# The memory cross-attention stage of a hybrid decoder step: seven half-block products for the query, sample values in four column strips, key rows fetched earlier

## The chip, the cores and the metric

The kernel runs on one core of one Trainium2 chip. Its time is the device time of one execution in microseconds (us). One launch computes everything; nothing is computed on the host.

## The reference, cut to what matters

One layer of a decoder serves a prompt (512 tokens) and eight sample sequences of four tokens (32 tokens) with the same weights. The 544 tokens go through every projection together. Everything is float32. The part that the change touches is the second residual step:

```python
def memory_attention(h, mk, mv, w_mq, w_mo):
    B, T, _ = h.shape
    q = (h @ w_mq).reshape(B, T, MEM_HEADS, MEM_HEAD_DIM)
    s = jnp.einsum('bthd,bmhd->bhtm', q, mk).astype(jnp.float32) * MEM_SCALE
    p = jax.nn.softmax(s, axis=-1).astype(mv.dtype)
    return jnp.einsum('bhtm,bmhd->bthd', p, mv).reshape(B, T, MEM_W) @ w_mo

x = x + memory_attention(rmsnorm(x, norm_mem_g), mk, mv, w_mq, w_mo)
```

The model width is 2048, and there are 4 memory heads of 128 over 256 memory tokens. The prompt's keys and values are computed from `mem_prompt` by `w_mk` and `w_mv`; each of the eight sample sequences reads its own from `cache_mem_k` and `cache_mem_v` (256 rows of 512 floats, 512 KB, for each sequence and kind). After this comes the gated feed-forward part (width 5632).

## The kernel before, in words

Every engine has its own instruction list, written out by hand, and the engines meet only at counting semaphores. So each engine works strictly in its own order, and whatever stands behind a waiting instruction waits too. Activations lie transposed, features on the 128 partitions and 544 tokens along the free dimension, cut into two halves of 272 tokens (`HALF`), because one PSUM bank holds 512 floats. A float32 matmul leaves two records in the trace.

Weights stream through a ring of four slabs of 1 MB (`RING`, semaphores `s_slab` when loaded and `s_used` when free). All loads of this stage are issued by SyncE, in program order: the four slabs of `w_mk`, of `w_mv`, of `w_mq` (line 857), of `w_mo` (line 861), each behind the use of the slab that it replaces; then the key rows of the eight sample sequences in two buffers `KMR` (line 867), then their value rows in six buffers `VMR` (line 874), then the small rows of the feed-forward part.

TensorE's order in the stage:

- the products for the prompt's keys and values (line 1512), each 64 matmuls of 512 columns, and two groups of transposes of the keys (line 920 is the helper of all transposes);
- the query product: `groups(1, SGR["mq"], ...)`, which for each of four 128-column slabs of `w_mq` runs 16 x 2 matmuls of 272 columns (line 925); ScalarE copies each result to `QM` (line 2026);
- `mem_scores(0)` (line 1540), `sample_keys(0)` (the transposes of the first sequence's keys, behind their load), `mem_scores(1)`, `sample_keys(1)`, `sample_scores(0)` (line 1581), and then for each of four blocks of 128 prompt tokens `mem_values` (transposes of the softmax), more sample keys and scores, and `mem_products` (line 1563);
- the softmax of the samples' scores and two transposes of it;
- the samples' value products (line 1625): for each of eight sequences, 4 heads x 2 halves of the memory, one matmul of 128 columns whose output is 32 partitions of a bank, the 32 partitions from `32 * (b % 4)` on; each sequence's products stand one behind the other. VectorE copies the bank of four sequences (line 2844), TensorE transposes it (`rows_out`), and ScalarE or VectorE copies that to `QM`;
- the output product by `w_mo` (line 1646), and on to the feed-forward part (line 956).

VectorE and ScalarE serve both streams. For `mem_scores(u)` VectorE takes the largest (`mem_largest`, line 2801), ScalarE the exponentials (`mem_exps`, line 2032), VectorE the scaling (`mem_scaled`, line 2807). Between these stand, in fixed places, the copies of the transposed sample keys (`keys_turned`, lines 1748 on ScalarE and 2154 on VectorE).

The input projection already uses, for three of its five groups, a Strassen-Winograd form: a product of a 2x2 block matrix of weights (two halves of the model width by two column tiles) with a 2x2 block matrix of activations (two halves of the width by two halves of the tokens) in seven half-block products instead of eight. `input_product` issues one of them (8 matmuls of 272 columns). Its sums are made by VectorE: of tokens in `QTS`, of weights by `input_weight_sums` in `QWS`; `input_first`, `input_middle` and `input_last` add up the results from PSUM, with the first copied by ScalarE to `QX`. Products rotate over six banks (`q_bank`), guarded by `s_qq` and `s_qx`.

## Time and profile before

| | us |
|---|---|
| median of 3 executions | 3250.27 (3248.58 to 3251.92) |
| the profiled execution, own time | 3249.63 |
| its span in the trace | 3248.0 |
| TensorE busy | 3139.9 |
| memory stage, last product of the output projection to first product by w_mo | 1261 to 1449 |
| query product in it | 58.9 |
| samples' value products in it | 13.1 busy |

The busy time of an engine is a share of the whole span; what a stage is worth is read from the timeline of that stage. The granted clock of TensorE over the whole execution is 0.988 of its full speed. The profiled execution's time lies 1.6 us above its span and 0.6 us below the median.

### The profile page before, as it was taken

The page shows a single profiled execution, that of the slowest core. Times are in us where ns is not written, and L with a number is a line of the kernel's source. Part 1 is how long each engine was busy: PE and PEld are TensorE (multiplying, and loading weights), DVE is VectorE, ACT ScalarE, POOL GpSimd, SP SyncE. Part 2 cuts the span into 40 slices and gives each one's busy share as a digit, 9 for nine tenths or more (in the row PEclk, how much of TensorE's full clock was granted, in tenths as well). Part 3 has the DMA queues.
Part 4 walks back from the last instruction along what each step waited for, and adds up shares of the span by engine and source line. Part 5 has one row for each costly group of instructions (what it writes and reads, how often), then busy time and mean ns, then how long its engine had stood idle before and what let it go on. Part 6 is the DMA issues. An engine that isn't in the chain of part 4 may idle for free.

```text
span 3248.0 us, 41139 instructions
## 1 busy us (share of the span) xinstructions
PE 3139.9 (97%) x14592; PEld 2528.6 (78%) x14592; DVE 1657.2 (51%) x3410; ACT 368.9 (11%) x899; POOL 77.8 (2%) x128
## 2 busy tenths in 40 slices
PE   8999999899888999989999999999999999999998
PEld 7788877788545886668888888888888888888876
DVE  7799232354556433136545544544454545455556
ACT  3000021111443002021000000000000000000013
POOL 0000000100012000000000000000000000000001
PEclk9999999999999999999999999999999999999999
DMA  7122223331118422631222321232232213213212
GB/s 229 53 77 67 79 66 105 118 122 48 52 30 284 156 79 95 226 123 66 90 65 72 107 81 58 84 104 77 65 92 89 90 52 103 83 55 108 86 49 94
DMA packets 299056, 306.92 MB, mean 94 GB/s; under 512 B 12680, under 2 KB 281612, under 8 KB 297023
## 3 DMA queue, kind: packets, MB, share of 16 engines
q1 hardware_dynamic: 293562, 280.38, 27.4%
q0 software_dynamic: 5376, 24.98, 2.2%
q8 instruction: 71, 1.16, 0.1%
q14 instruction: 47, 0.39, 0.0%
HBM read 291.36 MB, written 23.14 MB: 97 GB/s over the span
## 4 chain that ended last, share of the span: by engine, by line
PE 76%; DVE 2%; ACT 1%; issue 1%; DMA 0%; POOLq 0%; POOL 0%; DVEq 0%; SPq 0%; ACTq 0%
PE ps L956 58%; PE ps L1282 5%; PE ps L920 2%; PE ps L1646 2%; PE ps L925 2%; PE ps L1512 2%; PE ps L1321 1%; PE ps L1309 0%; PE ps L1310 0%; PE ps L1625 0%; ACT xT_region_b L1930 0%; PE ps L1251 0%; ACT xT_region_b L1748 0%; PE ps L1365 0%; PE ps L1563 0%
## 5 line engine op out<-in xcount | busy, mean ns | idle before, releaser
L956 PE MATMUL ps<-xT_region_b,weight_ring 128*128 128x272 f32 x2080 | 490.9, 392 | 1.1 <-DVE weight_ring L2186 1.1
L956 PEld LDWEIGHTS ps<-xT_region_b,weight_ring 128*128 128x128 f32 x2080 | 395.1, 190 | 82.9 <-issue 1.5
L956 PE MATMUL ps<-region_c,weight_ring 128*128 128x272 f32 x1664 | 401.4, 392 | 0.0
L956 PEld LDWEIGHTS ps<-region_c,weight_ring 128*128 128x128 f32 x1664 | 315.7, 190 | 65.3 <-issue 0.6
L925 PE MATMUL ps<-xT_region_b,weight_ring 128*128 128x272 f32 x1536 | 353.6, 393 | 2.7 <-DVE region_c L2154 1.1
L925 PEld LDWEIGHTS ps<-xT_region_b,weight_ring 128*128 128x128 f32 x1536 | 291.3, 190 | 63.6 <-issue 3.9
L956 PE MATMUL ps<-region_f 128*128 128x272 f32 x1408 | 336.9, 392 | 0.0
L956 PEld LDWEIGHTS ps<-region_f 128*128 128x128 f32 x1408 | 267.5, 190 | 55.1
L956 PE MATMUL ps<-region_f,weight_ring 128*128 128x272 f32 x960 | 229.9, 392 | 0.0
L1760 ACT ACTIVATE ext<-ps 128x272 f32<-128x272 f32 x100 | 39.7, 397 | 1625.9 <-PE ps L956 1614.0
L956 PEld LDWEIGHTS ps<-region_f,weight_ring 128*128 128x128 f32 x960 | 182.3, 190 | 37.7 <-issue 0.2
L2300 DVE SCALAR_TENSOR_TENSOR rstd<-ext,tile_taps,rstd 128x512 f32<-128x512 f32 x240 | 180.5, 752 | 8.5
L956 PE MATMUL ps<-region_c,region_f 128*128 128x272 f32 x704 | 177.4, 393 | 0.3 <-DVE region_f L2190 0.3
L956 PE MATMUL ps<-xT_region_b,v_tok 128*128 128x272 f32 x704 | 168.5, 392 | 0.0
L2212 DVE TENSOR_TENSOR ext<-ps,ext 128x272 f32<-128x272 f32 x100 | 44.1, 441 | 226.7 <-PE ps L956 226.7
L2210 DVE TENSOR_TENSOR ext<-ps,ext 128x272 f32<-128x272 f32 x100 | 44.1, 441 | 222.1 <-PE ps L956 222.0
L956 PEld LDWEIGHTS ps<-region_c,region_f 128*128 128x128 f32 x704 | 133.1, 190 | 29.5 <-issue 1.7
L956 PEld LDWEIGHTS ps<-xT_region_b,v_tok 128*128 128x128 f32 x704 | 133.8, 190 | 27.6
L956 PE MATMUL ps<-region_c,v_tok 128*128 128x272 f32 x480 | 119.1, 392 | 0.0
L920 PEld LDWEIGHTS ps<-consts,xT_region_b 128*128 128x128 f32 (+3 forms) x480 | 57.0, 145 | 65.1 <-issue 31.2
L956 PEld LDWEIGHTS ps<-region_c,v_tok 128*128 128x128 f32 x480 | 91.2, 190 | 18.8
L920 PE MATMUL ps<-consts,xT_region_b 128*128 128x128 f32 (+3 forms) x480 | 72.0, 290 | 31.9 <-ACT weight_ring L1748 10.6
(393 smaller groups left out, 3609.9 us busy)
## 6 DMA issues: line engine op xcount, KB each, us to landing
weight_ring<-in_w_ffn_gate SPq DMA_DIRECT2D x44, 1024.0 KB, 5.0
weight_ring<-in_w_ffn_up SPq DMA_DIRECT2D x44, 1024.0 KB, 5.0
weight_ring<-in_w_in SPq DMA_DIRECT2D x36, 1024.0 KB, 5.2
weight_ring<-in_w_ffn_down SPq DMA_DIRECT2D x64, 512.0 KB, 4.1
weight_ring<-in_w_out SPq DMA_DIRECT2D x16, 1024.0 KB, 5.3
weight_ring<-in_w_ffn_down SPq DMA_DIRECT2D x32, 384.0 KB, 3.7
region_f<-in_cache_k_cmp SPq DMA_DIRECT2D x64, 128.0 KB, 2.0
region_f<-in_cache_v_cmp SPq DMA_DIRECT2D x64, 128.0 KB, 2.0
```

Of the source, the lines that this page charges most:

```text
L920: return pe.transpose(dst, src, IDENT[0:n, 0:n])
L925: mm = pe.matmul(PS[:, 2 * j + h, 0:HALF], lhs(kt), rhs(kt, h), start=(kt == 0), stop=(kt == n - 1))
L956: mm = pe.matmul(prod(k, r), lhs[:, t, :], rhs[:, t, :], start=(t == 0), stop=(t == m - 1))
L1282: mm = pe.matmul(PS[:, 3 * f + r, 0:rhs.shape[1]], lhs, rhs, start=first, stop=last)
L1321: return pe.matmul(PS[:, 5, :], pieces[m][2], PT_[m][0:pieces[m][1], :], start=(m == 0), stop=(m == len(pieces) - 1))
L1512: mm = pe.matmul(PS[:, 2 * kind + tt, :], MT[:, kt, tt * P:(tt + 1) * P], w[:, a, :], start=(kt == 0), stop=(kt == KT - 1))
L1646: mm = pe.matmul(PS[:, n % 6, 0:HALF], w[:, kt, j * P:(j + 1) * P], QM[:, kt, h * HALF:(h + 1) * HALF], start=(kt == 0), stop=(kt == MH - 1))
L1760: act.activation(X1, prod(k, 0), ACT.Copy).then_inc(s_part, 1)
L2210: dve.tensor_tensor(U3, prod(k, 3), U2, ALU.add).then_inc(s_quad, 1)
L2212: dve.tensor_tensor(U4, prod(k, 4), U2, ALU.add).then_inc(s_quad, 1)
L2300: loop.tick(dve.scalar_tensor_tensor(out=RS[:, 0:SEQ], in0=E[:, w:w + SEQ], scalar=taps[:, w:w + 1], in1=RS[:, 0:SEQ], op0=ALU.mult, op1=A ...
```

## The change

1. The query product by `w_mq` is made by two pairs of seven half-block products (`query_pair`), with the helpers of the input projection, as its products 6 and 7. VectorE makes the sums of tokens (`MQT`, from the normed activations, one of them in place) and of weights (`MQW`) and adds up the results straight into `QM`; ScalarE makes two copies instead of four. The clearing of `QMP` moves behind this work.
2. The key rows of the first two sample sequences go to buffers of their own (`KMR`, at other places than before), and their loads are issued ahead of the slabs of `w_mq`. Those of the other six stay behind `w_mo`.
3. The value rows have eight buffers instead of six. The first six loads are issued behind the last key load, the last two behind all sample scores (they lie where the turned keys lie). The value products run head by head and half by half over four sequences in turn, in four column strips, and both turns to rows (`rows_out`) follow at the end.

```diff
-        KMR = [flat(RF, 4864 + 1024 * s, 2, MEMW) for s in range(2)]
+        KMR = [flat(RC, 9344, 2, MEMW), flat(EXA, 0, 2, MEMW)]
+        MQT = [flat(RF, 2176 * s, 8, HALF) for s in range(3)]
+        MQW = [flat(RF, 6528, 1024), flat(RF, 7552, 1024), flat(VTF, 0, 1024)]
+        QMEM = 6
-        VMR = [flat(RB, at, 2, MEMW) for at in (4096, 5120, 6144, 7168, 0, 1024)]
+        VMR = [flat(RB, at, 2, MEMW) for at in (4096, 5120, 6144, 7168, 0, 1024, 2048, 3072)]
...
+            def key_rows_in(b):
+                sp.dma_start(KMR[b % 2], A["cache_mem_k"][0, b].rearrange("(t p) h d -> p t (h d)", p=P)).then_inc(s_kmr[b % 2], 16)
+
+            key_rows_in(0)
+            sp.wait_ge(s_nac, KT - 1)
+            key_rows_in(1)
             for j in range(4):
                 sp.wait_ge(s_used[j], SGR["mq"])
...
+            for b in range(2, NB):
+                sp.wait_ge(s_tr, ms_at(b - 2) + 2)
+                key_rows_in(b)
+            sp.wait_ge(s_qp, PRODUCTS * (QMEM + 2))
             for b in range(NB):
...
-                if b >= 6:
-                    sp.wait_ge(s_mpv, QB + b - 5)
-                sp.dma_start(VMR[b % 6], ...).then_inc(s_vmr[b % 6], 16)
-
-            sp.wait_ge(s_mpv, QB + NB)
+                if b == 6:
+                    sp.wait_ge(s_mks, NB)
+                sp.dma_start(VMR[b], ...).then_inc(s_vmr[b // 4], 16)
+
+            sp.wait_ge(s_mpv, QB + 2)
...
+            pe.wait_ge(s_mke, 2)
+
+            def query_pair(k):
+                q, top, bottom = QMEM + k, RING[:, 2 * k, :], RING[:, 2 * k + 1, :]
+                pe.wait_ge(s_slab[2 * k], 16 * (SGR["mq"] + 1))
+                input_product(q, 0, top[:, 0:1024], lo[:, :, 0:HALF])
+                input_product(q, 1, top[:, 1024:2048], hi[:, :, 0:HALF])
+                pe.wait_ge(s_qsum, 6)
+                pe.wait_ge(s_qws, 4 * q + 2)
+                input_product(q, 2, MQW[1], MQT[1])
+                pe.wait_ge(s_slab[2 * k + 1], 16 * (SGR["mq"] + 1))
+                pe.wait_ge(s_qsum, 7)
+                pe.wait_ge(s_qws, 4 * q + 3)
+                input_product(q, 3, bottom[:, 0:1024], lo[:, :, HALF:TOK])
+                input_product(q, 4, MQW[0], MQT[0])
+                pe.wait_ge(s_qsum, 8)
+                input_product(q, 5, bottom[:, 1024:2048], MQT[2])
+                pe.wait_ge(s_qws, 4 * q + 4)
+                input_product(q, 6, MQW[2], hi[:, :, HALF:TOK], slabs=(2 * k, 2 * k + 1))
+
+            query_pair(0)
+            query_pair(1)
             turned(pe, end_of("memk"))
-            pe.wait_ge(s_mke, 2)
-            groups(1, SGR["mq"], PGR["mq"], KT, P, hrhs(HTL))
-            for j in range(4):
-                pe.wait_ge(s_ps[j], PGR["mo"])
+            pe.wait_ge(s_qx, QMEM + 2)
+            pe.wait_ge(s_qq, PRODUCTS * (QMEM + 2))
...
-            for b in range(NB):
-                pe.wait_ge(s_vmr[b % 6], 16 * (b // 6 + 1))
-                place = b % 4 * SAMP
+            for quarter in range(2):
+                pe.wait_ge(s_vmr[quarter], 64)
                 for h in range(MH):
                     for st in range(2):
-                        mm = pe.matmul(PS[place:place + SAMP, 2 + b // 4, ...], ..., VMR[b % 6][...], ...)
+                        for s in range(4):
+                            mm = pe.matmul(PS[s * SAMP:(s + 1) * SAMP, 2 + quarter, ...], ..., VMR[4 * quarter + s][...], ...)
                 mm.then_inc(s_mpv, 1)
-                if b == 4:
-                    rows_out(0)
+            rows_out(0)
             rows_out(1)
...
-            for j in range(4):
-                act.wait_ge(s_used[j], SGR["mq"] + 1)
-                act.activation(halves(QM[:, j, :]), PAIR[j], ACT.Copy).then_inc(s_ps[j], 1)
+            for q in (QMEM, QMEM + 1):
+                act.wait_ge(s_qq, PRODUCTS * (q - 1) + 2)
+                act.wait_ge(s_qp, PRODUCTS * q + 1)
+                act.activation(QX, q_bank(q, 0), ACT.Copy).then_inc(s_qx, 1)
...
             normed(KT, lambda kt: HTL[:, kt, :], lambda kt: XT[:, kt, :], lambda kt: VEC[:, kt, 1:2])
+            dve.wait_ge(s_h, HBASE["ffn"])
+            b11, b12, b21, b22 = [HTL[:, 8 * j:8 * j + 8, h * HALF:(h + 1) * HALF] for j in range(2) for h in range(2)]
+            dve.tensor_tensor(MQT[0], b12, b11, ALU.subtract).then_inc(s_qsum, 1)
+            dve.wait_ge(s_qsum, 5)
+            dve.tensor_tensor(MQT[1], b22, MQT[0], ALU.subtract).then_inc(s_qsum, 1)
+            dve.tensor_tensor(b12, b22, b12, ALU.subtract).then_inc(s_qsum, 1)
+            dve.wait_ge(s_qsum, 6)
+            dve.tensor_tensor(MQT[2], b21, MQT[1], ALU.subtract).then_inc(s_qsum, 1)
+            input_weight_sums(QMEM, MQW)
             turned_tiles("memk", mem_job)
-
+            input_first(QMEM)
+            input_middle(QMEM)
+            input_last(QMEM)
+            input_weight_sums(QMEM + 1, MQW)
+            input_first(QMEM + 1)
+            input_middle(QMEM + 1)
+            input_last(QMEM + 1)
             own.step(dve.memset(QMP, 0.0))
-            for j in range(4):
-                dve.wait_ge(s_ps[j], PGR["mo"])
+            dve.wait_ge(s_qq, PRODUCTS * (QMEM + 2))
```

## Rows read from the trace of the kernel before

**Rows 1.** Page of the profile: busy time by engine, and the chain that ended last.
```profile
PE 3139.9 (97%) x14592; PEld 2528.6 (78%) x14592; DVE 1657.2 (51%) x3410; ACT 368.9 (11%) x899; POOL 77.8 (2%) x128
...
PE 76%; DVE 2%; ACT 1%; issue 1%; DMA 0%; POOLq 0%; POOL 0%; DVEq 0%; SPq 0%; ACTq 0%
```

**Rows 2.** Timeline, TensorE, memory stage: start, duration, [idle before <- releaser].
```profile
1324.77 1.04 PE L920 MATMUL ps<-consts,region_c 128*128 128x128 f32 x8
1326.91 58.91 PE L925 MATMUL ps<-xT_region_b,weight_ring 128*128 128x272 f32 x256 [1.10 <-DVE region_c L2154]
1386.62 1.97 PE L1540 MATMUL ps<-region_c 128*128 128x256 f32 x8 [0.81 <-ACT region_c L2026]
1392.86 1.97 PE L920 MATMUL ps<-consts,region_f 128*128 128x128 f32 x8 [4.28 <-DMA region_f<-in_cache_mem_k]
1394.62 3.62 PE L1540 MATMUL ps<-region_c 128*128 128x256 f32 x8
...
1401.10 1.26 PE L920 MATMUL ps<-consts,region_f 128*128 128x128 f32 x8 [1.15 <-DVE region_f L2807]
...
1430.03 0.64 PE L1581 MATMUL ps<-xT_region_b,region_f 128*32 128x256 f32 x8
...
1433.61 8.52 PE L1625 MATMUL ps<-xT_region_b,region_f 128*32 128x128 f32 x80 [0.47 <-ACT region_f L1748]
...
1442.65 4.62 PE L1625 MATMUL ps<-xT_region_b,region_f 128*32 128x128 f32 x48
```

**Rows 3.** Stretches of TensorE: length, busy (records), granted clock, DMA share, GB/s.
```profile
367.00:418.60 51.60, 51.60 (x226) 1.00 0.28 82
1392.00:1398.30 6.30, 5.44 (x18) 0.50 0.41 141
1433.50:1436.20 2.70, 2.59 (x14) 0.50 0.00 0
```

**Rows 4.** Line 1414 alone (strips of the attention stage), same columns.
```profile
1024.58:1028.20 3.62, 3.62 (x132) 1.00 1.00 338
1042.40:1047.00 4.60, 4.58 (x88) 0.50 1.06 384
```

**Rows 5.** Timeline, VectorE, seven-product stretch of the input projection.
```profile
400.07 0.44 DVE L2371 TENSOR_TENSOR region_c<-ps,v_tok 128x272 f32<-128x272 f32 x1 [3.23 <-PE ps L1176]
400.43 1.22 DVE L2335 TENSOR_TENSOR region_c<-weight_ring 128x1024 f32<-128x1024 f32 x1
```

**Rows 6.** Timeline, VectorE, memory stage.
```profile
1301.84 11.22 DVE L2172 SCALAR_TENSOR_TENSOR xT_region_b<-xT_region_b,vecs,rstd 128x544 f32<-128x544 f32 x16
...
1326.70 0.91 DVE L2792 MEMSET region_f<- 128x1024 f32 x1 [0.16 <-issue]
...
1398.28 1.23 DVE L2801 TENSOR_REDUCE stats<-ps 128x4 f32<-128x1024 f32 x1 [2.72 <-PE ps L1540]
...
1399.82 1.23 DVE L2807 TENSOR_TENSOR region_f<-region_f,stats 128x1024 f32<-128x1024 f32 x1
...
1507.15 2.42 DVE L2890 TENSOR_TENSOR xT_region_b<-xT_region_b 128x2176 f32<-128x2176 f32 x1
```

**Rows 7.** Timeline, ScalarE, memory stage.
```profile
1324.97 1.03 ACT L2018 ACTIVATE region_c<-ps 128x1024 f32<-128x1024 f32 x1 [26.75 <-PE ps L1512]
...
1394.63 1.28 ACT L2032 ACT_TABLE_LOAD   x1
1395.92 0.47 ACT L2032 ACTIVATE region_f<-ps,stats 128x256 f32<-128x256 f32 x1
```

**Rows 8.** Timeline, SyncE's DMA issues: first issue, time to the last one, count.
```profile
1304.37 20.97 SPq L857 DMA_DIRECT2D weight_ring<-in_w_mq  x4
...
1386.26 32.51 SPq L867 DMA_DIRECT2D region_f<-in_cache_mem_k  x8
```

**Rows 9.** Issue to landing of the eight loads of sample value rows.
```profile
DMA to landing us min/median/max: 3.5/7.0/9.9
```

**Rows 10.** Issue to landing of the four slabs of w_mo.
```profile
DMA to landing us min/median/max: 4.9/9.0/25.1
```

More of the change, by code:

```diff
@@ L590, in hybrid_step @@
         s_kmr = [sem(f"memory_key_rows{k}") for k in range(2)]
-        s_vmr = [sem(f"memory_value_rows{k}") for k in range(6)]
+        s_vmr = [sem(f"memory_value_rows{k}") for k in range(2)]
         AT = flat(RC, 0, 8, TOK)
@@ L862, in _ @@
                              w_tiles(A["w_mo"][0])[:, :, j * 512:(j + 1) * 512]).then_inc(s_slab[j], 16)
+            for b in range(2, NB):
+                sp.wait_ge(s_tr, ms_at(b - 2) + 2)
+                key_rows_in(b)
+            sp.wait_ge(s_qp, PRODUCTS * (QMEM + 2))
             for b in range(NB):
[L865 to L876 removed]
+                if b == 6:
+                    sp.wait_ge(s_mks, NB)
+                sp.dma_start(VMR[b], A["cache_mem_v"][0, b].rearrange("(t p) h d -> p t (h d)", p=P)).then_inc(s_vmr[b // 4], 16)
+            sp.wait_ge(s_mpv, QB + 2)
             sp.dma_start(FR[0:16, :], A["state_ffn_conv"][0].rearrange("b t c -> (b t) c")).then_inc(s_fr, 16)
@@ L1618, in rows_out @@
                 ins.then_inc(s_tr, 1)
-            for b in range(NB):
-                pe.wait_ge(s_vmr[b % 6], 16 * (b // 6 + 1))
-                place = b % 4 * SAMP
+            for quarter in range(2):
+                pe.wait_ge(s_vmr[quarter], 64)
                 for h in range(MH):
                     for st in range(2):
-                        mm = pe.matmul(PS[place:place + SAMP, 2 + b // 4, h * DH:(h + 1) * DH], PMST[:, st, h * SAMP:(h + 1) * SAMP],
-                                       VMR[b % 6][:, st, h * DH:(h + 1) * DH], start=(st == 0), stop=(st == 1))
+                        for s in range(4):
+                            mm = pe.matmul(PS[s * SAMP:(s + 1) * SAMP, 2 + quarter, h * DH:(h + 1) * DH], PMST[:, st, h * SAMP:(h + 1) * SAMP],
+                                           VMR[4 * quarter + s][:, st, h * DH:(h + 1) * DH], start=(st == 0), stop=(st == 1))
                 mm.then_inc(s_mpv, 1)
-                if b == 4:
-                    rows_out(0)
+            rows_out(0)
             rows_out(1)
@@ L2325, in _, with input_weight_sums @@
             dve.tensor_tensor(QTS[1], b22, QTS[0], ALU.subtract).then_inc(s_qsum, 1)
-            def input_weight_sums(q):
-                g, k = q // 2 + 1, q % 2
+            def input_weight_sums(q, QWS=QWS):
+                k, group = q % 2, SGR["qkv"] + q // 2 + 1 if q < QMEM else SGR["mq"]
                 top, bottom = RING[:, 2 * k, :], RING[:, 2 * k + 1, :]
@@ L2331, in input_weight_sums @@
                 for j in range(2):
-                    dve.wait_ge(s_slab[2 * k + j], 16 * (SGR["qkv"] + g + 1))
+                    dve.wait_ge(s_slab[2 * k + j], 16 * (group + 1))
                 if q:
@@ L2344, in input_tiles @@
             def input_tiles(q):
+                if q >= QMEM:
+                    return [QM[:, 2 * (q - QMEM) + a, h * HALF:(h + 1) * HALF] for a in range(2) for h in range(2)]
                 return [C[:, 4 + 2 * q + a, h * HALF:(h + 1) * HALF] for a in range(2) for h in range(2)]
@@ L2789, in _ @@
             normed(KT, lambda kt: HTL[:, kt, :], lambda kt: XT[:, kt, :], lambda kt: VEC[:, kt, 1:2])
-            turned_tiles("memk", mem_job)
+            dve.wait_ge(s_h, HBASE["ffn"])
[7 more added lines that the diff above has]
+            input_weight_sums(QMEM, MQW)
+            turned_tiles("memk", mem_job)
+            input_first(QMEM)
[5 more added lines that the diff above has]
+            input_last(QMEM + 1)
             own.step(dve.memset(QMP, 0.0))
-            for j in range(4):
-                dve.wait_ge(s_ps[j], PGR["mo"])
+            dve.wait_ge(s_qq, PRODUCTS * (QMEM + 2))
             diag = bass.AP(RF, 3072, [[KT * TOK, P], [NB * SAMP, MH], [SAMP + NT, NB], [1, NT]])
@@ L2842, in _ @@
             for quarter in range(2):
-                dve.wait_ge(s_mpv, QB + 4 * quarter + 4)
+                dve.wait_ge(s_mpv, QB + quarter + 1)
                 dve.tensor_copy(MSV[:, quarter, :], PS[:, 2 + quarter, :]).then_inc(s_msv, 1)
```

6 lines of the change are left out of this document (removed).

## The prediction

> **What bounds the kernel now.** I read the page first: TensorE is busy for 3139.9 of 3248.0 us, and the chain that ended last runs for 76% of the span through it [rows 1]. VectorE is busy for half of that time. So the question for every edit is what it does to TensorE's own line. Then I read the timeline of TensorE in the memory stage. It shows what could be cut: 58.9 us of query product, a hole of 4.28 us in which TensorE waits for the first sample sequence's key rows, a shorter hole of 1.15 us before the first transposes of the softmax, and two runs of value products of 8.52 and 4.62 us [rows 2]. Third come the granted clocks of stretches: 1.00 for seven-product work, but 0.50, that is 1.2 GHz, after the hole of 4.28 us, and 0.50 again where the value products begin [rows 3]. Behind the stage stands a long unbroken line of products by w_mo and of the feed-forward part; what the stage saves is kept to the end, since those loads are issued relative to the products and not to an absolute time.
>
> **Seven products for eight.** Before: 256 records at 58.9/256 = 0.229 us each. The same kernel's seven-product stretch has 226 records in 51.6 us at clock 1.00 [rows 3], 0.228 us each, so neither the sums nor the hand-over between products cost TensorE anything there. After: 2 x 7 x 8 matmuls, 224 records, 51.3 us, which is 7.3 us less. This holds if the sums are in time:
> - Sums of tokens: four subtractions like line 2890 (128 x 2176, 2.42 us [rows 6]), 9.7 us, behind the normed tiles, which end at 1301.84 + 11.22 = 1313.1. They end at about 1322.8, while TensorE still makes the prompt's values.
> - Sums of weights of pair 0: four of 1.22 us [rows 5], so 1327.8. Slab 1 of w_mq was issued long before: the four issues begin at 1304.37 and end 20.97 us later [rows 8].
> - TensorE needs the first of them at product 2, two products (7.3 us) behind 1326.1, at 1333.4. Eight us to spare.
> - Pair 1's weight sums stand in VectorE's list behind the last addition of pair 0. That is about 0.5 us after its seventh product ends; two sums later (2.5 us) product 2 of pair 1 may begin, which it does after 7.3 us. Four us to spare.
> - Adding up is 14 operations of 0.44 us [rows 5] over 51 us.
> - VectorE copies the second group of turned prompt keys behind the weight sums, two us later than before. TensorE asks for that copy only after both pairs.
>
> Two small terms. TensorE began the query product at 1326.91, released by VectorE's copy of the turned keys. That wait now stands behind the pairs. What is left is ScalarE's copy of the values, 1324.97 + 1.03 = 1326.0 [rows 2, 7], so it begins at about 1326.1: 0.8 us less. At the end TensorE waited 0.81 us for ScalarE's copy [rows 2]; now it waits for an addition of 0.44 us with about 0.2 us of hand-over, 0.15 us less. The clearing of QMP (0.91 us [rows 6]) now comes after that addition, under the first scores (1.97 us [rows 2]), and only the first sample scores need it: nothing.
>
> **Key rows ahead.** Let t = 0 be the end of the query product. Before, the first transposes of the softmax began at 1401.10, t = 15.3. In between lie the hole and the low clock behind it: eight transposes took 1.97 us and the second scores 3.62 us, where the first took 1.97 [rows 2, 3]. After, both key loads are issued before w_mq's, that is before 1304.37, and the old first load took 1392.86 - 1386.26 = 6.6 us [rows 2, 8]. They have landed 70 us before use. Even those 6.6 us do not push a slab of w_mq: it was issued 20 us ahead of use. The new chain:
> - first scores t = 0.65 to 2.6, keys 0 turned by 3.5, second scores 3.4 to 5.3, TensorE not waiting;
> - VectorE: largest(0) 2.65 to 4.1, turned keys to 4.8, largest(1) from 5.3. From the start of largest(1) to the end of the first scaling it took 1398.28 to 1401.05, 2.8 us [rows 6], and will again if the exponentials are there: t = 8.1;
> - ScalarE: turned keys at 2.9 to 3.6, its table load of 1.28 us to 4.85, four exponentials of about 0.47 us [rows 7] to 6.8. This is 0.2 us later than the scaling would like: t = 8.3, and transposes begin at 8.4.
>
> So 15.3 - 8.4 = 6.9 us; the exponentials of block 1 then run about 0.4 us later relative to the transposes than before, which I charge at 0.2: 6.7 us. Bounds: 5.5 us (the table load or a second wait not hidden) and 7.2. Key rows 2 now are issued when the first keys are turned, t = 3.9, and at 3.6 to 6.6 us land by 10.5; they are wanted about 1.4 us behind the first softmax transposes, at t = 9.8. Most likely in time, and 0.7 us is the bound.
>
> A rule of the Trainium skill bears on the table load. The row shows it for 1.28 us and the first exponential starting at its end, 1394.63 to 1395.92 [rows 7]. The skill (ScalarE: Activation LUTs, What ACT_TABLE_LOAD costs) states about 1.28 us for the load and a drain of about 1.38 us, 2.66 us per switch. By it the exponentials would be 1.4 us later and the gain here 5.3 us; the trace shows no such drain, and the sum goes by the row.
>
> **Values in four strips.** Before: 128 records from 1433.61 to 1442.65 + 4.62 = 1447.3, 13.7 us with the turn in the middle [rows 2]. The nearest row is line 1414, the same shape (128 x 32 weights, 128 columns) in the same strip order: 132 records in 3.62 us at clock 1.00, 0.027 us each, and 88 in 4.58 us at 0.50, 0.052 us [rows 4]. All at full clock 3.5 us, all at half 6.7 us. Before, the clock was 0.50 here for the first 2.7 us [rows 3]; nothing ahead of it changes, so I take that again: 52 records in the first 2.7 us, 76 in 2.05 us, with 0.3 us for the last to drain: 5.1 us. That saves 8.6 us, between 6.7 and 9.9. The tail behind them is the same (copy, turn, copy); the turn of the first four sequences falls into the wait for the second copy.
> Are the value rows there? The first six loads keep their place, behind the last key load. Loads 6 and 7 now wait for the last sample scores, 1430.03 + 0.64 = 1430.7 [rows 2]. At the least 3.5 us each [rows 9] and a further 1.4 us for the second (512 KB at the 384 GB/s of [rows 4]): about 1436.0. The second four sequences begin 2.7 us and a bit behind 1433.6, at 1436.5. Just in time; with the longest landing, 9.9 us [rows 9], 4.5 us too late.
> SyncE's other moves: w_mo's slabs are issued later for 0 and 2, at about 1349 and 1374.5 instead of 15 us apart; the longest landing was 25.1 us [rows 10], and their use begins after 1425. Nothing.
>
> **Sum.** 7.3 + 0.8 + 0.15 + 6.7 + 8.6 = 23.5 us. The profiled execution took 3249.6 us: 3226.1. The median of the runs shown is 0.6 us higher, inside their spread. **I predict 3226 us**, its own range 3223 to 3229.
>
> **The rivals.**
> - *A gain given back to the clock.* The stretches behind the query product become shorter and emptier, and 0.50 was granted after gaps twice. If it is 0.50 through second scores and first transposes (3.62 - 1.9 and 1.97 - 1.04: 2.6 us), all value products (6.7 for 5.1) and the first 3 us of w_mo's (1.5 us), 5.7 us are lost: 3232. For it: the value stage was cold before with a gap of under 2 us. Against: no gap of more than 1.7 us is left in the first stretch.
> - *Late value rows.* Loads 6 and 7 at 9.9 us: +4.5, 3230.6. Against: that landing belonged to six loads issued together.
> - *The strips do not overlap*, so that part of the change does nothing: 8.6 less, 3234.7. Rows 4 against.
> - *VectorE late with the sums of tokens or weights in each pair*, giving back the 7.3 us: 3233.4. Against: the spare 8 and 4 us.
> - *Slower: the fourteen products run at 1.2 GHz.* Their 51.3 us would double, 3249.6 - 23.5 + 51.3 = 3277.4. It decides from 47 us at the low clock, where the loss of half of them eats 23.5. Against: 1.00 over 51.6 us of just such products [rows 3].
> - *No change*: TensorE not the bound in the stage. Against: its chain [rows 1].
>
> **How the numbers follow.** Forecast 0.66, the clock 0.12, late rows 0.09, strips 0.03, sums 0.05, slower 0.02, no change 0.03. A difference of 0.2%, 6.5 us, is about what a measurement of this kernel can tell from none. Faster in all but the last two: 0.95, same 0.03, slower 0.02. The range for 8 in 10 takes in the better bounds (7.2 and 9.9: 1.8 us more) with the runs' spread below, and the first two rivals above: 3223 to 3232.5.
>
> **What would show it.** Right: 224 records of 0.229 us in the query product with no idle time between; transposes of the softmax at t = 8.4 with no release by a DMA; 128 value records in about 5 us, the second half without a wait. Wrong: a release of TensorE by a weight or token sum, by ScalarE's exponentials well past t = 8.4, by the landing of value rows, or a granted clock of 0.50 in new places.

## The result and the profile after

| | before | changed |
|---|---|---|
| median | 3250.27 us (5 runs, 3248.58 to 3253.07) | 3229.24 us (4 runs, 3226.51 to 3230.43) |
| ratio | | 0.9931, 95% interval 0.9918 to 0.9943 |
| profiled execution, own time | 3249.63 | 3230.43 |
| its span | 3248.0 | 3228.8 |

The change makes the kernel faster by 0.7%. A fifth execution of the changed kernel took 3348.93 us with a granted clock of 0.94 over all of it; it is left out here. With the eleven further ones of e0 and e10 (below) the median is 3228.4 us, from 3225.27 to 3239.26; without the highest it would be 3227.8.

The page of the changed kernel, busy time of TensorE and the others, and the chain that ended last, to set beside [rows 1]:

```profile
PE 3124.9 (97%) x14560; PEld 2514.8 (78%) x14560; DVE 1682.0 (52%) x3436; ACT 366.8 (11%) x897; POOL 77.8 (2%) x128
...
PE 76%; DVE 2%; ACT 1%; issue 1%; DMA 0%; POOLq 0%; POOL 0%; DVEq 0%; SPq 0%; ACTq 0%
```

TensorE lost 15.0 us of busy time and 32 records, and the chain is still its own.

TensorE's timeline in the memory stage, changed kernel (start, duration, idle before and its releaser), to set beside [rows 2]:

```profile
1327.25 1.04 PE L926 MATMUL ps<-consts,region_c 128*128 128x128 f32 x8
1328.58 7.57 PE L1182 MATMUL ps<-xT_region_b,weight_ring 128*128 128x272 f32 x32 [0.29 <-issue]
...
1376.32 3.83 PE L1182 MATMUL ps<-xT_region_b,v_tok 128*128 128x272 f32 x16
1380.78 1.97 PE L1566 MATMUL ps<-region_c 128*128 128x256 f32 x8 [0.63 <-DVE region_c L2399]
1382.58 1.04 PE L926 MATMUL ps<-consts,region_c 128*128 128x128 f32 x8
1383.45 1.89 PE L1566 MATMUL ps<-region_c 128*128 128x256 f32 x8
...
1388.58 1.26 PE L926 MATMUL ps<-consts,region_f 128*128 128x128 f32 x8 [1.80 <-DVE region_f L2849]
...
1420.98 3.97 PE L1651 MATMUL ps<-xT_region_b,region_f 128*32 128x128 f32 x128 [0.47 <-ACT region_f L1773]
1424.88 0.66 PE L926 MATMUL ps<-consts,region_f 128*128 128x128 f32 x4
1425.76 0.66 PE L926 MATMUL ps<-consts,region_f 128*128 128x128 f32 x4 [0.23 <-DVE region_f L2886]
1426.73 33.27 PE L1671 MATMUL ps<-region_c,weight_ring 128*128 128x272 f32 x144 [0.31 <-ACT region_c L1773]
...
1473.68 2.91 PE L926 MATMUL ps<-consts,region_f 20*128 20x20 f32 x44
...
1494.68 5.41 PE L962 MATMUL ps<-xT_region_b,weight_ring 128*128 128x272 f32 x16 [1.12 <-DVE weight_ring L2212]
```

Four things are to be seen. The first of the seven-product records stands 1.33 us behind the start of the last turn of the prompt's keys, where it was 2.14. The fourteen products follow each other without idle time from 1328.58 to 1380.15. The transposes of the first sample keys (1382.58) and the second scores (1383.45) wait for nothing. And the 128 value records are one run of 3.97 us, with both turns behind it. That run is not quite free of waits: TensorE's weight loads waited 0.33 us for the value rows of the second four sequences.

```profile
1423.00 1.69 PEld L1651 LDWEIGHTS ps<-xT_region_b,region_f 128*32 128x32 f32 x64 [0.33 <-DMA xT_region_b<-in_cache_mem_v]
```

Granted clocks of stretches of the changed kernel (length, busy, clock, DMA share, GB/s), to set beside [rows 3]:

```profile
1327.00:1380.00 53.00, 52.71 (x233) 1.00 0.75 253
1383.20:1389.80 6.60, 4.80 (x36) 1.00 0.61 203
1420.90:1426.70 5.80, 5.15 (x136) 1.00 0.66 163
1476.00:1484.00 8.00, 8.00 (x35) 0.79 0.42 150
```

It is 1.00 in the query product, through second scores and first softmax transposes, and in the value products, where before it was 0.50 twice; but 0.79 in a stretch of w_mo's products, where before it was 1.00.

VectorE in the changed kernel, the last sum of tokens, and the first and last weight sum of pair 0; then the last addition of pair 0 and the first two weight sums of pair 1:

```profile
1322.72 2.42 DVE L2825 TENSOR_TENSOR region_f<-xT_region_b,region_f 128x2176 f32<-128x2176 f32 x1
1325.06 1.22 DVE L2361 TENSOR_TENSOR region_f<-weight_ring 128x1024 f32<-128x1024 f32 x1
...
1328.59 1.22 DVE L2368 TENSOR_TENSOR v_tok<-weight_ring,region_f 128x1024 f32<-128x1024 f32 x1
```

```profile
1354.52 0.44 DVE L2399 TENSOR_TENSOR region_c<-ps,v_tok 128x272 f32<-128x272 f32 x1 [3.23 <-PE ps L1182]
1354.88 1.22 DVE L2361 TENSOR_TENSOR region_f<-weight_ring 128x1024 f32<-128x1024 f32 x1
1356.13 1.23 DVE L2363 TENSOR_TENSOR region_f<-region_f,weight_ring 128x1024 f32<-128x1024 f32 x1
```

ScalarE, its table load and first exponential, to set beside [rows 7], and SyncE's issues (first issue, time to the last, count), to set beside [rows 8]:

```profile
1383.83 1.28 ACT L2058 ACT_TABLE_LOAD   x1
1385.12 0.47 ACT L2058 ACTIVATE region_f<-ps,stats 128x256 f32<-128x256 f32 x1
```

```profile
1299.47 0.51 SPq L859 DMA_DIRECT2D region_c<-in_cache_mem_k  x1
1300.03 0.47 SPq L859 DMA_DIRECT2D ext<-in_cache_mem_k  x1
1306.85 20.97 SPq L866 DMA_DIRECT2D weight_ring<-in_w_mq  x4
1351.31 26.59 SPq L870 DMA_DIRECT2D weight_ring<-in_w_mo  x4
1383.64 0.37 SPq L859 DMA_DIRECT2D region_c<-in_cache_mem_k  x1
...
1406.28 12.81 SPq L880 DMA_DIRECT2D xT_region_b<-in_cache_mem_v  x8
```

To compare executions I cut TensorE's line into stretches, each from the start of one record of the timeline to the start of another, so that a shift from earlier drops out. "Query" runs from the prompt keys' last turn to the first scores, "keys" on to the first softmax transposes, "blocks" to the first value product, "values" to the first product by w_mo, "w_mo" to the first product of the feed-forward part. "Stage" is all from the first product for the prompt's keys to the first by w_mo.

```
kernel                 query   keys  blocks  values   stage    w_mo    span
before                 61.85  14.48   32.51   15.41  180.17   66.26  3248.0
before, second profile 61.82  13.52   32.40   14.18  177.84   66.25  3247.3
changed                53.53   7.80   32.40    5.75  155.40   67.95  3228.8
changed, e0            53.52   7.80   32.41    7.15  156.81   66.25  3223.6
changed, e10           53.52   7.81   32.40    5.69  155.34   67.95  3227.5
e1 eight products      61.81   7.81   33.51    5.86  164.91   67.94  3235.9
e2 keys late           53.52  11.31   32.40    7.15  160.31   66.25  3226.7
e3 values in turn      53.52   7.80   32.39   13.07  162.71   67.94  3236.8
e4 sums late           58.34   7.80   32.40    7.15  161.61   66.26  3230.4
e5 value loads free    53.52   7.81   32.40    7.15  156.80   66.26  3225.8
e7 three small         53.52   7.43   32.40    5.48  154.76   66.56  3226.8
e8 split only          53.52   7.81   32.40    5.83  155.48   66.55  3224.1
e9 three small, again  53.52   7.43   32.41    7.15  156.43   66.55  3225.7
```

The stage is 24.77 us shorter in the changed kernel's profile than in the one of before, the span only 19.2. The difference is told by stretches too: the stage began 2.48 us later (the low clock lies in other places ahead of it, in work that the change doesn't touch: over 1062 to 1066 us it is 0.50 where the profile of before has 1.00, over 827 to 836 us 0.81 where that has 0.62), w_mo's stretch is 1.69 us longer, and what follows 1.40. The last is the first feed-forward products: 16 records in 5.41 us, at a mean clock of 0.72 over 1494.7 to 1500.1, where before they took 3.90 at 1.00. In a second profile of the same kernel, e0, the stage is 23.36 us shorter and the span 24.4. So single spans are worth a few microseconds. Stretches repeat to a tenth or two where the clock is the same, but a low clock in one moves it by 1 to 1.7 us: keys 14.48 and 13.52 and values 15.41 and 14.18 in the two profiles of before, values 5.75 and 7.15 in those of the changed kernel.

### The profile page after: what moved, and what is told of

Its sections match the earlier page's. It is cut to its first block, busy times and chain, and to the rows that moved or that the text cites. A ratio compares the mean times of both kernels' runs of the same rounds, so it can differ in the third digit from the quotient of the medians.

```text
span 3228.8 us, 41116 instructions
## 1 busy us (share of the span) xinstructions
PE 3124.9 (97%) x14560; PEld 2514.8 (78%) x14560; DVE 1682.0 (52%) x3436; ACT 366.8 (11%) x897; POOL 77.8 (2%) x128
## 4 chain that ended last, share of the span: by engine, by line
PE 76%; DVE 2%; ACT 1%; issue 1%; DMA 0%; POOLq 0%; POOL 0%; DVEq 0%; SPq 0%; ACTq 0%
PE ps L962 59%; PE ps L1288 5%; PE ps L926 2%; PE ps L1671 2%; PE ps L1518 2%; PE ps L1182 2%; PE ps L1327 1%; PE ps L1315 1%; PE ps L1316 0%; ACT xT_region_b L1955 0%; ACT xT_region_b L1773 0%; PE ps L1257 0%; PE ps L1420 0%; PE ps L1371 0%; PE ps L1589 0%
## 5 line engine op out<-in xcount | busy, mean ns | idle before, releaser
L962 PE MATMUL ps<-xT_region_b,weight_ring 128*128 128x272 f32 x2080 | 492.5, 393 | 1.1 <-DVE weight_ring L2212 1.1
L962 PEld LDWEIGHTS ps<-xT_region_b,weight_ring 128*128 128x128 f32 x2080 | 396.2, 191 | 83.4 <-issue 1.5
L931 PE MATMUL ps<-xT_region_b,weight_ring 128*128 128x272 f32 x1280 | 294.7, 393 | 1.6 <-ACT region_f L1773 1.0
L931 PEld LDWEIGHTS ps<-xT_region_b,weight_ring 128*128 128x128 f32 x1280 | 242.7, 190 | 52.3 <-issue 2.6
L1182 PE MATMUL ps<-xT_region_b,weight_ring 128*128 128x272 f32 x480 | 113.7, 393 | 0.3 <-issue 0.3
L1182 PEld LDWEIGHTS ps<-xT_region_b,weight_ring 128*128 128x128 f32 x480 | 91.1, 190 | 19.2 <-issue 0.5
```

Source lines behind the costliest of these rows:

```text
L931: mm = pe.matmul(PS[:, 2 * j + h, 0:HALF], lhs(kt), rhs(kt, h), start=(kt == 0), stop=(kt == n - 1))
L962: mm = pe.matmul(prod(k, r), lhs[:, t, :], rhs[:, t, :], start=(t == 0), stop=(t == m - 1))
L1182: mm = pe.matmul(q_bank(q, r), lhs[:, t * P:(t + 1) * P], rhs[:, t, :], start=(t == 0), stop=(t == 7))
```

## The experiments

All of them start from the changed kernel; e0 and e10 are that kernel unchanged, and b1 is the kernel before. Kernels that ran together on one chip share their runs of the kernel before.

### The changed kernel again (e0)

> The changed kernel once more, to see what varies. In its first profile the stage from the first product of the prompt's keys to the first product by w_mo took 155.4 us, against 180.2 before: 24.8 us less, while the whole execution was only 19.2 us shorter. Theory: the other 5.6 us are stretches of granted clock 0.50 that fall in other places from execution to execution; so the stage repeats within 0.5 us, the 14.79 us for the last 56 records of w_mo's products go back to about 13.1 in some executions, and the median over the fast runs lies 21 to 25 us under before. Rival: the change itself gives gain back behind the stage, so that those 56 records take about 14.8 us again, with 0.50 in the same place, and the median is 19 to 21 us under before.

Median 3228.37 us (3225.29 to 3231.12) against 3250.97: 0.9933, 0.9919 to 0.9946. It is the base for e1 to e3. The expectation that the stage repeats within 0.5 us was missed: it took 156.81 us against 155.40, since the value products ran at a lower clock. The 56 records behind the small transposes did go back, from 14.79 to 13.10 us.

### e1: the query product by eight half-block products

```diff
-            query_pair(0)
-            query_pair(1)
             turned(pe, end_of("memk"))
-            pe.wait_ge(s_qx, QMEM + 2)
-            pe.wait_ge(s_qq, PRODUCTS * (QMEM + 2))
+            pe.wait_ge(s_mke, 2)
+            groups(1, SGR["mq"], PGR["mq"], KT, P, hrhs(HTL))
+            for j in range(4):
+                pe.wait_ge(s_ps[j], PGR["mo"])
```

With it go VectorE's sums, and ScalarE makes its four copies again.

> The query product as it was, by eight half-block products with ScalarE's copies, all else as changed. Theory (TensorE's line is the bound, the sums are hidden): the stage takes 155.4 + 8.3 = 163.7 us, 256 records in the query product, and the time lies 8 us (7 to 9.5) over the changed kernel's. Rival (the sums on VectorE cost something in later work that the query stretch doesn't show): the stage grows by less than 7 us. Rival (clock): the whole time grows by less than 5 us although the stage grows by 8.

Median 3237.59 us (3237.01 to 3242.45), ratio 0.9962 (0.9949 to 0.9975), 9.2 us over e0. TensorE's timeline in e1:

```profile
1328.40 58.91 PE L932 MATMUL ps<-xT_region_b,weight_ring 128*128 128x272 f32 x256 [1.06 <-DVE region_c L2160]
1388.11 1.97 PE L1547 MATMUL ps<-region_c 128*128 128x256 f32 x8 [0.81 <-ACT region_c L2032]
...
1429.43 1.95 PE L1632 MATMUL ps<-xT_region_b,region_f 128*32 128x128 f32 x64 [0.47 <-ACT region_f L1754]
1431.56 1.95 PE L1632 MATMUL ps<-xT_region_b,region_f 128*32 128x128 f32 x64 [0.17 <-DMA xT_region_b<-in_cache_mem_v]
```

The product takes 58.91 us again, behind a wait of 1.06 for VectorE's copy and ahead of one of 0.81 for ScalarE's, and the query stretch is 61.81 against 53.53: 8.28 us. The stretches behind it are those of the changed kernel but for a clock of 0.62 over 1395.8 to 1400.3 (1.1 us). So the seven-product form gave 8.28 us, all of it in its own stretch; that its sums or its moved waits cost something elsewhere falls.

The last row also shows how close the value rows were: here TensorE waited 0.17 us for them at the second four sequences, until 4.9 us behind the last sample scores (1431.56 against 1425.97 + 0.64), and its weight loads waited 0.43 us. At full clock "just in time" was missed by a few tenths: the weight loads waited 0.33 us in the changed kernel's first profile and 0.27 us in e10.

### e2: the first key rows loaded where they were

```diff
-            key_rows_in(0)
             sp.wait_ge(s_nac, KT - 1)
-            key_rows_in(1)
...
-            for b in range(2, NB):
-                sp.wait_ge(s_tr, ms_at(b - 2) + 2)
+            for b in range(NB):
+                if b >= 2:
+                    sp.wait_ge(s_tr, ms_at(b - 2) + 2)
                 key_rows_in(b)
```

> The first two key loads are issued behind w_mo's slabs again, all else as changed. Theory: TensorE waits for them again. The last slab of w_mo is now issued about 3 us ahead of the end of the query product, and two slabs of 1 MB stand directly in front of the keys, so the keys land 7 to 10 us behind their issue at about 1378.3 on the changed kernel's clock, the hole before the first transposes of keys is 3 to 6 us, 0.50 is granted behind it, and the softmax transposes begin 6 to 9 us later: stage 161.5 to 164.5 us. Rival (only the transfer is moved, the gain came from the earlier end of the query product): the hole is under 1 us, the stage under 157 us.

Four executions: 3228.38, 3237.82, 3229.04 and 3238.32 us; ratio 0.995 (0.9935 to 0.9965). The profile is of the first. TensorE's timeline and two stretches of e2:

```profile
1382.27 1.09 PE L925 MATMUL ps<-consts,region_c 128*128 128x128 f32 x8 [3.30 <-DMA region_c<-in_cache_mem_k]
1383.20 1.89 PE L1565 MATMUL ps<-region_c 128*128 128x256 f32 x8
```

```profile
1380.30:1382.20 1.90, 0.00 (x0) 1.00 1.06 411
1383.20:1389.50 6.30, 4.51 (x34) 1.00 0.47 166
```

The hole is back, 3.30 us, released by the key rows, but the records behind it ran at full clock: eight transposes in 1.09 us where before they took 1.97 [rows 2]. The keys stretch is 3.51 us longer than with the change, and I had expected 6 to 9. Of the 6.68 us that the change took from this stretch, then, about half is the hole; the rest is the low clock that in both profiles of before stood behind it (and 1 us more of hole), and that this hole of 3.30 us, with loads at 411 GB/s in it, did not bring. The clock varies between executions of one kernel too: b1, the kernel before profiled again, had a hole of 4.22 us and 0.72 over 1394.3 to 1400.5 behind it, and 13.52 us instead of 14.48. The two executions of 3238 us, at mean clocks of 0.986 and 0.987 against 0.990, have no profile. Whether the low clock was in their keys stretch stays open, and so does more than 9 us between the groups.

### e3: value products one sequence behind the other

```diff
-                for h in range(MH):
-                    for st in range(2):
-                        for s in range(4):
+                for s in range(4):
+                    for h in range(MH):
+                        for st in range(2):
```

> The value products one sequence after the other again, within each four sequences; buffers, loads and both turns at the end stay as changed. Theory (the strips overlap in the array): the 128 records take 12.3 us at full clock (0.096 each) or 13.5 us with 0.50 at their beginning, instead of 3.97, and the stage 163.7 to 165.2 us. Rival (the gain came from the clock of 1.00 in this stretch or from no longer having the turn in the middle): the records take under 8 us.

Median 3238.03 us (3235.33 to 3239.73), ratio 0.9958 (0.9943 to 0.9973), 9.7 us over e0. TensorE's timeline in e3:

```profile
1423.44 11.31 PE L1651 MATMUL ps<-xT_region_b,region_f 128*32 128x128 f32 x128 [0.47 <-ACT region_f L1773]
```

```profile
1423.40:1436.50 13.10, 12.56 (x136) 1.00 0.27 68
```

The same 128 records, with the same buffers, loads and turns, take 11.31 us in this order and 3.97 in the other, both at a granted clock of 1.00: 0.088 us each against 0.031. The 3.97 us still hold the wait for value rows. In e7 (below), where no record waits for them, the 128 took 3.70 us, and without the last record's own 0.27 us that is 0.027 each; in turn it is 0.087. I had expected 12.3 us, from 0.096 each. The order of three loops is worth 7.3 us; buffers and merged turns are worth the rest (13.07 against 14.18 in b1, where the clock was full here too). That the strips do not overlap, or that the eight buffers made the gain, falls.

### e4: the weight sums of pair 1 made late

```diff
-                pe.wait_ge(s_qsum, 8)
+                pe.wait_ge(s_qsum, 8 + 3 * k)
...
+            for n in range(3):
+                dve.wait_ge(s_qsum, 8 + n)
+                dve.tensor_tensor(MQT[2], b21, MQT[1], ALU.subtract).then_inc(s_qsum, 1)
             input_weight_sums(QMEM + 1, MQW)
```

Three superfluous sums of 128 x 2176 stand ahead of them, to test how many microseconds VectorE had to spare.

> Three more token subtractions of 2.42 us (repeats of the fourth) stand on VectorE ahead of the weight sums of the second pair: 7.3 us. In the changed kernel those sums began 0.2 us behind the last product of pair 0 and the second was ready 2.5 us later, 4.3 us before product 2 of pair 1 wanted it. Theory: TensorE waits 7.3 - 4.3 = 3.0 us once, ahead of product 2 of pair 1, released by the second weight sum, and 53.5 us from the turned prompt keys to the first scores become 56.5. Rival (VectorE has far more spare time than that, the products don't depend on it closely): under 1 us. Rival (no spare time): 7 us.

One execution, 3232.07 us. VectorE's timeline, then TensorE's with two stretches:

```profile
1353.60 7.33 DVE L2833 TENSOR_TENSOR region_f<-xT_region_b,region_f 128x2176 f32<-128x2176 f32 x3
...
1362.11 1.23 DVE L2363 TENSOR_TENSOR region_f<-region_f,weight_ring 128x1024 f32<-128x1024 f32 x1
```

```profile
1363.44 5.59 PE L1182 MATMUL ps<-region_f 128*128 128x272 f32 x16 [2.90 <-issue]
```

```profile
1357.00:1363.40 6.40, 3.54 (x16) 1.00 0.75 260
1363.40:1368.80 5.40, 5.36 (x16) 0.68 0.76 287
```

The three sums took 7.33 us on VectorE, and TensorE waited 2.90 us. Its row names no releaser ("issue"), but the second weight sum ended at 1363.34, 0.1 us before it went on. So the spare was 7.33 - 2.90 = 4.4 us where the prediction had 4. But the stretch is 4.82 us longer, not 2.90: the 16 records behind the wait ran at a mean clock of 0.68, for 5.59 us instead of 3.83. In this kernel a wait of 2.9 us in full work cost 1.7 times its length, once; the hole of 3.30 us in e2 cost its own length alone.

### e5: the last two value loads not behind the scores

```diff
-        VMR = [flat(RB, at, 2, MEMW) for at in (4096, ..., 2048, 3072)]
+        VMR = [flat(RB, at, 2, MEMW) for at in (4096, ..., 0, 1024)] + [flat(RF, 4864, 2, MEMW), flat(RF, 5888, 2, MEMW)]
...
-                if b == 6:
-                    sp.wait_ge(s_mks, NB)
```

> The last two sample value loads go to a free place, so that they no longer wait for the last sample scores: all eight are issued in one line. In the changed kernel the eighth landed as the first four sequences' products ended, and TensorE's weight load waited 0.3 us. Theory: that wait goes, and the loads are no bound; from the first value product to the first by w_mo 5.7 us at full clock or 7.1 with 0.50, as before within 0.3 us. Rival (eight loads in one line, 4 MB, crowd each other and the first four land later): TensorE waits over 1 us ahead of the first value product.

One execution, 3227.51 us. All eight loads are issued by 1409.6, none is waited for, and the values stretch is 7.15, as in e0. But both are profiles with a low clock in this stretch, and there e0 has no wait for value rows either. At full clock the loads do bind a little: with this edit in it, e7's stretch is 5.48 us where the others at full clock have 5.69 to 5.86.

### b1: the kernel before again

> The kernel before once more, for what varies in its stretches. Theory (places of granted clock 0.50 change from execution to execution): the stretch of the second scores with the hole in front stays 14.5 us or drops to about 12 where 0.50 doesn't follow the hole; the value stretch is 15.4 us or about 14; w_mo's stretch 66.3 or 67.9. Rival (the places are fixed for a kernel): all stretches as in its first profile within 0.3 us, and 1.7 us in w_mo's stretch is then a cost of the change.

One execution, 3249.0 us; its line is in the table. The value products ran at full clock here, and the stretch is 1.23 us shorter than in the first profile. The low clock did follow the hole again, for less time, and w_mo's stretch took 66.25 us: 0.50 was granted neither in the value products nor there.

### e7 and e9: three small edits together

```diff
+            act.activation(SSM[:, 0:1], cst("eps"), ACT.Exp)
             def mem_exps(u):
...
-                if n == 24:
-                    (44 transposes of 20 x 20, two groups of 22)
+                if n in (23, 25):
+                    (22 of them)
```

The first loads ScalarE's exponential table under the query product, the second splits a run of tiny transposes inside w_mo's products, and the third is e5's. The second was made because in the changed kernel w_mo's stretch is low in clock right behind that run.

> Three small edits together, each read in its own stretch: the eight value loads in one line as in the run with free buffers; a dummy exponential on ScalarE behind the last copy of the query product, so that the table load of 1.28 us falls there; and the 44 small transposes for the feed-forward part in two runs of 22, two products apart, in the stretch where two of three profiles of kernels with the change showed the granted clock at 0.50. Theory: from first scores to softmax transposes 7.8 - 0.2 = 7.6 us, since the largest of block 1 ends 0.3 us behind the exponentials' end; w_mo's stretch 66.3 us, without 0.50 in it, where 67.9 was seen; the time 0 to 2 us under the changed kernel. Rival on the table load: 1.3 us less in the first stretch, as the exponentials alone decide. Rival on the clock: the low stretch has nothing to do with the small transposes, and w_mo's stretch takes 67.9 us again.

Median 3227.46 us (3226.67 to 3229.36), ratio 0.9928 (0.9914 to 0.9942). ScalarE's timeline in e7, and TensorE's first softmax transposes:

```profile
1360.23 1.28 ACT L2050 ACT_TABLE_LOAD   x1
...
1385.81 0.47 ACT L2056 ACTIVATE region_f<-ps,stats 128x256 f32<-128x256 f32 x1 [0.43 <-DVE stats L2842]
```

```profile
1389.78 1.26 PE L924 MATMUL ps<-consts,region_f 128*128 128x128 f32 x8 [1.42 <-DVE region_f L2847]
```

The load is gone from the path: the first exponential waits 0.43 us for VectorE's largest value, no longer for the table. Counted from the first scores the exponentials begin 0.88 us earlier than in the changed kernel (1385.81 - 1382.35 against 1385.12 - 1380.78), and the transposes 0.37 us earlier (7.43 for 7.80, where 0.2 was expected): VectorE's largest of block 1 now stands ahead of the scaling. The rival by which the load cost all of its 1.28 us falls.

> The three small edits together once more. Theory: as in their first profile, 7.4 us from the first scores to the softmax transposes, 5.5 us (7.0 with 0.50) in the value stretch, 66.6 us in w_mo's; time 1 to 2 us under the changed kernel in the same call. Rival: the same time as the changed kernel within 0.5 us, and 67.9 us in w_mo's stretch.

Median 3227.42 us (3227.1 to 3229.41), ratio 0.9931 (0.9918 to 0.9943): the 0.37 us are there again (7.43), and as a whole the edits can't be told from no change.

### e8 and e10: the split alone, beside the changed kernel

> The changed kernel with one edit: the 44 small transposes in w_mo's stretch in two runs of 22, two products apart. So far 0.50 was granted in w_mo's stretch of the changed kernel in some profiles (67.9 us) and in the value stretch in the others (7.1 us instead of 5.7), never in both. Theory (the run of 44 is what lets it fall in w_mo's stretch): 66.3 to 66.6 us there, never 67.9, whatever the value stretch shows; time 0 to 1.5 us under the changed kernel. Rival (chance alone: the low stretch falls where it falls): 67.9 us there in this profile or the next one with the split.

> The changed kernel a third time, beside the two others on one chip. Theory: 7.8 us from scores to softmax transposes; either 5.7 us in the value stretch with 67.9 in w_mo's, or 7.1 with 66.3; median 21 to 24 us under before. Rival (no link between the two places): 7.1 with 67.9, or 5.7 with 66.3.

e8: median 3225.79 us (3225.64 to 3227.72), ratio 0.9925 (0.9912 to 0.9938). e10: 3228.23 (3225.27 to 3239.26), 0.9937 (0.9923 to 0.995). The intervals overlap, so e8's lead of 2.4 us isn't shown by the times. TensorE's w_mo stretch in e8, then the clock of the value products and of w_mo's stretch in e8, and then in e0:

```profile
1470.97 1.54 PE L926 MATMUL ps<-consts,region_f 20*128 20x20 f32 x22
...
1476.31 1.54 PE L926 MATMUL ps<-consts,region_f 20*128 20x20 f32 x22
1477.78 11.27 PE L1671 MATMUL ps<-region_c,weight_ring 128*128 128x272 f32 x48
```

```profile
1420.00:1425.80 5.80, 5.15 (x136) 1.00 0.62 160
1425.90:1492.40 66.50, 64.30 (x308) 1.00 0.14 44
```

```profile
1417.60:1424.80 7.20, 6.62 (x137) 0.76 0.49 127
1424.80:1491.00 66.20, 64.04 (x308) 1.00 0.14 44
```

In e0 the value products are low (0.76) and w_mo's stretch is full (66.25 us). In the first profile of the changed kernel it is the other way round: values full, 44 transposes in 2.91 us at 1473.68, and 0.79 behind them (67.95 us). Among the eight profiles that have the whole run of 44 and the change in some form, four are of the one kind and four of the other, and none has both or neither. With the run split, w_mo's stretch was 66.55 all three times, and in two of them (e7, e8) the values were at full clock too, a pair that didn't occur in the eight. That suggests that the low clock in w_mo's stretch hangs on the unbroken run of tiny transposes. One pair of profiles makes it a fair comparison: ahead of the stage e8 and e10 were granted the same clocks (1.00, 0.72, 0.79, 0.72, 0.63 and 0.64 over 827 to 836, 846 to 852, 880 to 888, 938 to 950, 1034 to 1048 and 1058.5 to 1068 us), and both had full clock in the value products. Then e10, unsplit, took 67.95 us for w_mo's stretch and 5.47 for the first 16 feed-forward records, and e8, split, 66.55 and 3.90. That is 3.0 us of the 3.4 us between their spans. It isn't proven: these are two executions, and b1, with the run unsplit, had full clock in both places. So the run alone does not bring the low clock.

## Why the prediction was right

The forecast was 3226 us with 3223 to 3229 as its own range, and the measured median of 3229.24 lies 0.24 above that range and inside the wide one, 3223 to 3232.5; the 3228.4 with e0 and e10 lies in both. Step by step:

- **Start and end waits.** 0.8 us forecast at the start, 2.14 - 1.33 = 0.81 measured. VectorE's moved copy of the turned keys (1329.72) delayed nobody.
- **Seven products.** 7.3 forecast, 58.91 - (1380.15 - 1328.58) = 7.34 measured. The prediction's 58.9/256 is 0.230 and not 0.229, and the 51.3 us that it gave for the fourteen products were 51.6; the 7.3 in the sum doesn't depend on that. At the end 0.15 forecast, 0.81 - 0.63 = 0.18 measured. The three make the 8.32 us of the query stretch, and e1 gives back 8.28 by undoing them.
- **Sums in time.** The tokens' last sum was forecast to end at about 1322.8, with TensorE at 1326.1. It ended at 1325.1 with TensorE at 1328.6: 3.3 us apart as forecast, 3.4 as measured. Spare for pair 1: 4 forecast, 4.4 by e4.
- **Key rows.** Transposes of the softmax forecast at 8.4 us behind the query product's end; 1388.58 - 1380.15 = 8.43. But t counts from the end of the query product, so its 15.3 and 8.4 hold the end wait, and I had booked its 0.15 us twice. The charge of 0.2 us for the exponentials of block 1 was not seen either: "blocks" became 0.11 shorter. The two errors cancel, which is luck: 6.68 + 0.11 = 6.8 us measured for the 6.7 forecast. The gain was put down to the hole and to the low clock behind it, and that this clock comes with the hole each time was my reading of one profile. e2 shows a hole of 3.30 us without it, and against b1 the stretch saved 5.72 us.
- **The table load.** The Trainium skill (ScalarE: Activation LUTs, What ACT_TABLE_LOAD costs) would have a drain of 1.38 us beside the load, by which this part would have been 5.3 us. Here the first exponential starts 1.29 us after the load does (1383.83 and 1385.12), so the sum by the row holds.
- **Value strips.** 8.6 us forecast, from 5.1 us of value products. Measured: 3.97 at full clock in one profile, 5.37 where the clock was low in another (e0, e2). Clock for clock, the stretch saves 15.41 - 7.15 = 8.26 with low clock before and after, and 14.18 - 5.75 = 8.43 with full clock in both. The price of [rows 4] held, 0.027 us a record at full clock (e7, by e3's reckoning): all at full clock the sum gives 3.5 + 0.3 = 3.8, and the record shows 3.97 with the wait for value rows and 3.70 without. At the low clock it is 0.3 more than the 5.1, since more of it than the 2.7 us booked ran at 0.50. The prediction's assumption "nothing ahead of it changes, so I take that again" held for some executions and not for others, in either kernel; it was a draw, not a property of the code. The landing of the last value rows was forecast 5.3 us behind the last scores, though its terms, 3.5 and 1.4, make 4.9; the weight loads went on 4.9 us behind them in e1 and in the changed kernel. They still waited, because at full clock the first four sequences were done earlier than the sum had them.
- **Where the rest is.** The medians fell by 21.0 us here, 22.6 in e0 and 22.0 in e10, for 23.5 forecast. What the stage saves depends on which profiles are set side by side: 23.36 to 24.83 us against the first profile of before, 21.03 to 22.50 against b1, 23.2 on average over the six pairs. The forecast took both low stretches of the first profile as certain, so it lies at the high side of that, and that e0 against the first profile fits to 0.2 is luck. The spans of the changed kernel's first profile and e0 differ by 5.2 us: 3.34 of it arose ahead of the stage, in work that the change doesn't touch, the stage takes 1.41 back, w_mo's stretch adds 1.70 and what follows 1.57, nearly all in the first feed-forward products. So each of the four profiles with the change that had full clock in the value products gave those 1.4 us back in w_mo's stretch, and two of them 1.5 us more behind it. The first rival had priced such a loss at 5.7 us, as an alternative to the whole forecast; it is a small term that comes and goes, 0.3 to 1.8 us net.

Rivals: late value rows (a wait of 0.27 to 0.43 us of the weight loads at full clock, none at the low one, for 4.5 us priced), strips that don't overlap (e3), VectorE late (e4), products at 1.2 GHz (1.00 over all of them) and no change are all contradicted by rows. What stays open: what decides where the clock falls in one execution, and the two executions of e2 at 3238 us.

## What to carry to other kernels

Price each part of a change in its own stretch, between two records that stand in both kernels: here parts of 8.3 and 8.4 us could be read to a tenth or two between profiles with the same clock there, while spans of the same kernel differ by 5 us. The third part, 6.7 us in one profile of before and 5.7 in the other, shows the limit: it held a stretch of low clock. When a low clock stands behind a hole in one profile, profile the same kernel once more before that clock goes into the sum as a certainty. And look for matmuls that fill only a part of the array and stand in turn: issuing four of them on four strips was a reordering of loops worth 7.3 us of 11.3.

## What the runs showed of the hardware

- Matmuls of 128 x 32 weights and 128 columns, float32, cost 0.087 us a record when consecutive ones write the same 32 partitions (e3) and 0.027 when four strips take turns and nothing is waited for (e7), both at a clock of 1.00 and without the last record's own time: a factor of 3.2, not 4.
- A wait of TensorE of 2.90 us was followed by a mean clock of 0.68 over 5.4 us (e4), one of 3.30 us by 1.00 (e2), one of 4.22 us by a mean of 0.72 over 6.2 us (b1), one of 4.28 us by 0.50 over 6.3 us (before). The length of the wait alone doesn't order these.
- The exponential's table load is issued ahead of its operands: it began at 1383.83, while the largest value that the exponential needs was ready at 1384.21 (VectorE's largest of block 0 ends 1384.00, and its scaling starts 1384.04 and takes 0.17), so 0.38 us of the load was hidden without any edit, and e7, which moves the load away, starts the exponentials 0.88 us earlier, about the rest of the 1.28.
